# Inverse root of a group norm: as a square root on ScalarE and a reciprocal on VectorE, or as a power on GpSimd

## What is computed

```python
def rms_norm(x, g):
    xf = x.astype(jnp.float32)
    y = xf * lax.rsqrt(jnp.mean(xf * xf, axis=-1, keepdims=True) + NORM_EPS)
    return (y * g.astype(jnp.float32)).astype(x.dtype)

def memory_attention(q, mem, mem_norm_g, w_kv, q_gain, k_gain):
    k, v = jnp.split(rms_norm(mem, mem_norm_g) @ w_kv, 2, axis=-1)
    k = rms_norm(split_heads(k), k_gain)
    v = split_heads(v)
    q = rms_norm(q, q_gain)
    logits = jnp.einsum('bshd,bmhd->bhsm', q, k).astype(jnp.float32) / math.sqrt(HEAD_DIM)
    probs = jax.nn.softmax(logits, axis=-1)
    return jnp.einsum('bhsm,bmhd->bshd', probs.astype(v.dtype), v)

def dilated_attention(q, k_blocks, v_blocks, q_gain, rel_bias, seq_len):
    q = rms_norm(q, q_gain)
    ...
```

## Time and profile before

| | before |
|---|---|
| runs, median of 3 | 3174.85 us (3172.94 to 3175.13) |
| profiled execution | 3173.09 us |
| its span in the trace | 3171.3 us |
| TensorE busy | 3118.1 us, 98% |
| VectorE busy | 1709.1 us, 54% |
| ScalarE busy | 1208.3 us, 38% |
| GpSimd busy | 477.7 us, 15% |
| granted TensorE clock, mean | 0.996 |

### The profile page before, as it was taken

The page is one execution under the profiler, slowest core; times in us unless marked ns, Lnnn a source line. Parts: engine busy times, 40 slices in busy tenths (PEclk is TensorE's granted clock), DMA queues, the critical chain, the costliest instruction groups (busy, mean ns, idle before and its releaser), DMA issues.

```text
span 3171.3 us, 43885 instructions
## 1 busy us (share of the span) xinstructions
PE 3118.1 (98%) x18144; PEld 2475.1 (78%) x18144; DVE 1709.1 (54%) x2547; ACT 1208.3 (38%) x1923; POOL 477.7 (15%) x407
## 2 busy tenths in 40 slices
PE   9999999999999999999999999999999999999999
PEld 7777678877777888887777788888878887678887
DVE  6965556845456443347877544335474334554433
ACT  4355534535552422234344432223252224542221
POOL 0022112003110311113222021111001001021110
PEclk8999999999999999999999999999999999999999
DMA  6765233436331323333200033333323323033232
GB/s 247 246 188 141 67 107 121 122 112 169 101 107 60 93 94 99 96 116 104 67 3 2 34 113 113 100 94 99 94 87 98 95 92 92 15 97 97 96 100 80
DMA packets 103497, 321.62 MB, mean 101 GB/s; under 512 B 10488, under 2 KB 26116, under 8 KB 101124
## 3 DMA queue, kind: packets, MB, share of 16 engines
q1 hardware_dynamic: 80564, 275.82, 27.4%
q10 hardware_dynamic: 22736, 43.00, 5.1%
HBM read 311.41 MB, written 9.72 MB: 101 GB/s over the span
## 4 chain that ended last, share of the span: by engine, by line
PE 86%; DVE 4%; ACT 3%; issue 1%; POOL 0%; DMA 0%; ACTq 0%; DVEq 0%; POOLq 0%
PE acc L498 72%; PE acc L1600 1%; PE acc L2623 1%; PE acc L2609 1%; PE aux L1911 1%; PE aux L1922 1%; PE acc L1935 1%; PE acc L2110 1%; PE aux L2099 1%; PE aux L3411 1%; DVE ssd_ex L1497 1%; DVE w_lo L409 0%; ACT w_hi L402 0%; PE aux L230 0%; PE aux L3443 0%
## 5 line engine op out<-in xcount | busy, mean ns | idle before, releaser
L498 PE MATMUL acc<-op_hi,w_hi 128*128 128x512 f32 x2624 | 1068.3, 407 | 5.1 <-DVE op_lo L1230 2.0
L402 ACT ACTIVATE w_hi<-raw 128x1024 fp32r<-128x1024 f32 (+2 forms) x476 | 494.2, 1038 | 1469.1 <-PE acc L498 1458.3
L498 PE MATMUL acc<-op_lo,w_hi 128*128 128x512 f32 x2624 | 1024.7, 391 | 0.0
L498 PE MATMUL acc<-op_hi,w_lo 128*128 128x512 f32 x2624 | 1024.6, 390 | 0.0
L409 DVE TENSOR_TENSOR w_lo<-raw,w_hi 128x1024 fp32r<-128x1024 f32 (+2 forms) x476 | 577.3, 1213 | 250.6 <-ACT w_hi L402 250.2
L498 PEld LDWEIGHTS acc<-op_hi,w_hi 128*128 128x128 f32 x2624 | 493.7, 188 | 145.9 <-issue 47.0
L498 PEld LDWEIGHTS acc<-op_lo,w_hi 128*128 128x128 f32 x2624 | 494.2, 188 | 105.4 <-issue 9.8
L498 PEld LDWEIGHTS acc<-op_hi,w_lo 128*128 128x128 f32 x2624 | 493.3, 188 | 105.9
L498 PE MATMUL acc<-ffn_hi,w_hi 128*128 128x512 f32 x800 | 311.4, 389 | 0.0
L498 PE MATMUL acc<-ffn_hi,w_lo 128*128 128x512 f32 x800 | 311.2, 389 | 0.0
L498 PE MATMUL acc<-ffn_lo,w_hi 128*128 128x512 f32 x800 | 311.2, 389 | 0.0
(11 more groups left out here) (615 smaller groups left out, 3535.5 us busy)
## 6 DMA issues: line engine op xcount, KB each, us to landing
raw<-in_w SPq DMA_DIRECT2D x436, 512.0 KB, 3.6
late_ada<-in_ada ACTq DMA_DIRECT2D x32, 512.0 KB, 4.3
raw<-in_w SPq DMA_DIRECT2D x32, 384.0 KB, 3.1
ssd_ex<-cum ACTq DMA_DIRECT2D x16, 512.0 KB, 5.4
ssd_ex<-cum ACTq DMA_DIRECT2D x16, 384.0 KB, 6.1
ada<-in_ada ACTq DMA_DIRECT2D x4, 1024.0 KB, 14.2
ada<-in_ada SPq DMA_DIRECT2D x4, 1024.0 KB, 23.0
ssd_ex<-cum ACTq DMA_DIRECT2D x16, 256.0 KB, 5.2
```

Source lines behind the costliest of these rows:

```text
L402: act.activation(self.w_hi[g % AHEAD][:, 0:k, :], self.raw[s][:, 0:k, :], ACT.Copy).then_inc(self.split_hi.handle, 1)
L498: mm = pe.matmul(self.bank(s, g), w[:, k, :], a[:, k, 0:s.n], start=(k == 0 and q == 0), stop=(k == k_tiles - 1 and q == 2))
```

## The change

ScalarE's instruction at L3318 keeps its place, its waits, its operands and the added constant, but its function is Identity in place of Sqrt. VectorE's reciprocal at L3359 is taken out. In its place GpSimd waits for the same semaphore and raises the factor to the power of minus one half, with an exponent that is read from a new 128x1 tile `minus_half`; this instruction now signals `inverted`. It stands in GpSimd's program at the planned time at which the reciprocal stood in VectorE's. The new tile is set once, at the start, by VectorE. Other norms of the kernel keep square root and reciprocal.

```diff
@@ Startup.dve, first_weights
             dve.memset(core.norm_eps[:, :], EPS).then_inc(*self.eps_set.inc())
+            dve.memset(core.minus_half[:, :], -0.5)
             dve.memset(self.idle_tile[:, :], 1.0).then_inc(*self.idle_set.inc())
@@ GroupNorms.act, roots
-                act.activation(self.factor[:, 0:P], self.sums[:, 0:P], ACT.Sqrt, bias=self.eps
+                act.activation(self.factor[:, 0:P], self.sums[:, 0:P], ACT.Identity, bias=self.eps
                                ).then_inc(*self.rooted.inc())
@@ GroupNorms
     def dve(self, dve):
         def work():
             for j, g, i, src, n in self.tiles():
-                if i == 0:
-                    yield self.at[j + n - 1] + 4.2
-                    dve.wait_ge(*self.rooted.ge(g + 1))
-                    dve.reciprocal(self.factor[:, 0:P], self.factor[:, 0:P]).then_inc(*self.inverted.inc())
                 yield self.spread_at(j, g, i, n) + 1.0
                 dve.wait_ge(*self.spreaded.ge(j + 1))
                 self.finish(dve, j, self.spread[:, :]).then_inc(*self.made.inc())
         return (work(),)
+
+    def pool(self, pool):
+        def roots():
+            for j, g, i, src, n in self.tiles():
+                if i == 0:
+                    yield self.at[j + n - 1] + 4.2
+                    pool.wait_ge(*self.rooted.ge(g + 1))
+                    pool.tensor_tensor(self.factor[:, 0:P], self.factor[:, 0:P], column(self.core.minus_half[:, 0:1]), ALU.pow
+                                       ).then_inc(*self.inverted.inc())
+        return (roots(),)
@@ build
         core.mem_k, core.mem_v = ([core.sb(f"mem_{n}{i}", [P, 2, MEM]) for i in range(DEPTH)] for n in "kv")
+        core.minus_half = core.sb("minus_half", [P, 1])
         core.norm_small, core.norm_eps = core.sb("norm_small", [P, 3 * NT]), core.sb("norm_eps", [P, 1])
```

## The result

The changed kernel takes 3245.69 us (median of 4 runs, 3242.99 to 3247.67) against 3174.31 for the kernel before: 71.4 us more, a ratio of 1.0225 with a 95% interval of 1.0207 to 1.0242. The profiled execution took 3247.67 us, with a span of 3245.9.

The account below looks back on a forecast made before the run. TensorE, busy 98% of the span, was taken to bound the kernel. The profiled 3173.09 us less 1.8 of TensorE idle time gave 3171.3, and 3173.0 for the median, 1.8 above the profiled run; range 3169.5 to 3200.

Parts of the forecast that it names:

- The sign most held: Whole kernel: a change within 0.2%, 6.3 us, held at 0.59, against slower 0.38 and faster 0.03.
- the price of the power: GpSimd's 128x128 power at four group norms: near 3 us, between 1.7 and about 3.4, range left open upward.
- The removals: Four table loads go; only the third late group's pair counts, ending TensorE's 1.76 us pause: 1.8 us, between 0.9 and 3.5.
- The covers: Time for the power before TensorE's spread: 3.7 us first late group and memory attention, 8.1 second, 3.3 third.
- Rival A: Slow power makes TensorE wait at the spreads, then the clock falls; chance 0.05 from 4.2 us to the mark, 0.38 past.
- its formula: Net loss at the four spreads for power time T: 3T - 12.5 over 3.7 us, 4T - 20.6 from 8.1 us.
- The clock's condition: Behind TensorE's waits at the spreads: stalls over 1.5 us bring the clock down, costing up to 1.8 us a time.
- The dependent steps: GpSimd's power: 0.43 us a dependent step for 128 elements; some 8 steps fit the cover, 14 pass 6 us.
- a price of the first power alone: First of GpSimd's four powers: code that must be fetched would show as one long row; no size given.
- a slower VectorE beside it: VectorE's instructions beside a running GpSimd power might slow down; no size given.

Follow-up runs that it names:

- the product's kernel: The changed kernel with a plain product by minus one half on GpSimd in place of the power: 3170.34 us against 3173.78 for the kernel before, ratio 0.999.

## Why the prediction was wrong

The forecast was 3173.0 us, between 3169.5 and 3200, and the time is 3245.69. The sign most held (no change that can be told) was wrong, and the time lies 46 us past the range.

- **The failed step is the price of the power**, T, "near 3" us. It measured 20.7. I took VectorE's reciprocal at six times a product's time for each element, and doubled it; on GpSimd the power is 0.159 us a column, eighty times the 2.0 ns a column that I had for the product. (The product itself, taken at 0.44 us, measured 0.40.) No row of the kernel before bounded T from above. I said so, and still ended the range at T = 10.5.
- The removals: right. No load at the group norms' line, two fewer in front of the exponentials, and only the third late group on the path. Sized at 0.9 to 3.5 us and taken at 1.8, they measured 3.4 with the power out of the way (interval of the ratio 0.9981 to 0.9999).
- The covers: right at three places. 20.7 less waits of 17.0, 17.0 and 12.84 leaves 3.7, 3.7 and 7.9, against 3.7, 3.7 and 8.1. At the third late group the wait of 18.73 leaves 2.0 where I drew 3.3. I had drawn it with TensorE's work at the lower clock. In the changed kernel that work ran at a granted clock of 1.00 (scores 1.04 us where the earlier trace rows has 1.52, turns 0.66 for 1.18), and TensorE stood at the spread sooner; in the product's kernel, where the clock did fall, the cover is 3.0 us (2731.20 to 2734.24).
- Rival A: its mechanism held, waits and then the clock. With the measured T its formula gives 62.3 us, and its clock, "up to 1.8 us a time", adds 7.2, so 69.5 against 71.4. That this is so near is in part luck. The waits were 65.6 us where the formula has 64.1, the removals won 3.4 and not 1.8, and what neither explains, 3245.69 - 3170.34 - 65.6 = 9.8 us, is more than 7.2. The result lies past 3200, to which I gave 0.15.
- The clock's condition was wrong: "Stalls of over 1.5 us would also bring the clock down behind them, as happened after the pause of rows 4". In the earlier trace rows it stands at 0.71 ahead of the pause, and in the product's kernel it falls at that place without one. Stalls of 1.7, 1.7 and 2.65 us left it at 1.00; those of 6.65 us and more are the ones with slow work behind them. At the measured T all four were such, so this did not cost the sum.
- The dependent steps that the Trainium skill prices ("GPSIMD Engine Reference", section Performance pitfalls for Q7 kernels) pointed the right way. At its four cycles for a step, the measured 0.159 us a column, 191 cycles of 1.2 GHz, would be 48 dependent steps (an estimate); no run shows what the routine does inside.
- The other doubts: a price of the first power alone does not exist here (20.735 us against 20.715 to 20.731), and a slower VectorE beside it was not found.

## What to carry to other kernels

An operation that no row of the trace shows has no upper bound from rows of other operations: from VectorE's reciprocal the power came out near 3 us, and it took 20.7. The range has to stay open to it, or the change should be judged by its break-even, here 4.2 us by the formula, and the chance that the operation stays under it. A table load is worth the idle time of the bounding engine behind it, not its 1.28 us; of four loads here two counted. A stall of TensorE costs its length; here those of 7 to 19 us cost some 2 us more at the lower clock, and two of 1.7 us and one of 2.65 did not bring the clock down.

## What the runs showed of the hardware

A power on GpSimd takes 0.3 to 0.4 us and 0.159 us for each column, whether 32 or 128 partitions hold data and whether its exponent is one repeated number or a full tile; a product of the same 128x128 takes 0.40 us. A power of 20.7 us beside VectorE, ScalarE and TensorE added no time that can be told (3173.39 us against 3173.78). Logarithm and exponential in alternation brought a table load of 1283 ns each time. Behind a stall of 13 to 19 us, TensorE's granted clock stood at 0.50 for some 4 to 6 us of work, and it stood at 0.50 behind stalls of 6.7 us too; behind stalls of 1.7 and 2.65 us it stood at 1.00. With idle products through the long stalls it stood at 1.00 and the whole was 6.9 us shorter.
